# Moving the weight-only half of a Hyena mixer into an earlier feed-forward stage

## The reference, cut to what matters

```
h = _rms_norm(x, norm_mlp_pre[l])                       # first block, end of layer l (l = 0, 1)
u = square(relu(h @ w_up[l]))                           # 256 x 4096
x = x + _rms_norm(u @ w_down[l], norm_mlp_post[l])

feats, t = hyena_position_features(seq)                 # 256 x 33: constants
hdn = sin(freq * (feats @ w1 + b1)); hdn = sin(freq * (hdn @ w2 + b2)); hdn = sin(freq * (hdn @ w3 + b3))
h = (hdn @ w_out) * exp(-t * abs(deltas))               # 256 x 4096: 2 orders x (fwd, bwd) x 1024 channels
fwd, bwd = h[:, :, 0], h[:, :, 1]
circ = concatenate([fwd, zeros, flip(bwd[1:])])         # 512 lags
filt = circ / (sum(abs(circ)) + RMS_EPS)

proj = x @ w_in; x1, x2, v = dwconv_centred(xv); gate    # Hyena mixer
z = x1 * (fft_long_conv(v, filt[:, 0]) + skip[0] * v)    # product of spectra, length 512
y = x2 * (fft_long_conv(z, filt[:, 1]) + skip[1] * z)
return y * silu(gate)
```

## Time and profile before

| | us |
|---|---|
| median of the runs | 1590.55 |
| the profiled execution's own time | 1594.65 |
| its span, first to last instruction | 1593.3 |
| TensorE busy | 1495.4 (94%) |
| VectorE busy | 1060.4 (67%) |
| ScalarE busy | 777.4 (49%) |

### The profile page before, as it was taken

How to read it: one execution, slowest core, us unless ns; L and a number is a source line. 1 busy time by engine, 2 the same in 40 slices (tenths; PEclk the granted TensorE clock), 3 DMA queues, 4 the chain that set the end, 5 groups by cost and what they waited for, 6 DMA issues and landing times.

```text
span 1593.3 us, 27504 instructions
## 1 busy us (share of the span) xinstructions
PE 1495.4 (94%) x11820; PEld 1319.0 (83%) x11820; DVE 1060.4 (67%) x1830; ACT 777.4 (49%) x1318; POOL 51.7 (3%) x58
## 2 busy tenths in 40 slices
PE   7999999999999998989999999897789999999998
PEld 7888898899989998988999898886678878885566
DVE  5576666655564776656555586757467668977877
ACT  4656444544454565445445566343242436746435
POOL 0001011000000010110000000000000000000000
PEclk9999999999999999989999999998779799999999
DMA  8554344565546543434655564200000266432143
GB/s 274 182 179 137 106 133 146 181 221 197 185 159 190 187 141 115 133 121 150 205 186 195 175 217 129 86 26 1 1 2 3 108 213 190 144 107 66 53 127 131
DMA packets 151190, 219.13 MB, mean 138 GB/s; under 512 B 6228, under 2 KB 110684, under 8 KB 150428
## 3 DMA queue, kind: packets, MB, share of 16 engines
q1 hardware_dynamic: 151068, 217.37, 42.0%
HBM read 216.29 MB, written 1.06 MB: 136 GB/s over the span
## 4 chain that ended last, share of the span: by engine, by line
PE 72%; DVE 16%; ACT 8%; DMA 2%; issue 1%; SPq 0%; DVEq 0%; ACTq 0%
PE bank L396 18%; PE bank L398 18%; PE bank L397 18%; DVE weights_low L372 4%; PE bank L3684 2%; ACT weights_high L359 2%; PE bank L2200 1%; PE bank L2158 1%; PE bank L898 1%; PE bank L2095 1%; PE bank L3694 1%; DMA place<-w_in_dram 1%; PE bank L3705 1%; DVE place L1240 1%; PE bank L2402 1%
## 5 line engine op out<-in xcount | busy, mean ns | idle before, releaser
L372 DVE TENSOR_TENSOR weights_low<-place,weights_high 128x1024 fp32r<-128x1024 f32 (+2 forms) x387 | 449.3, 1205 | 165.7 <-ACT weights_high L359 165.1
L359 ACT ACTIVATE weights_high<-place 128x1024 fp32r<-128x1024 f32 (+2 forms) x387 | 378.7, 1032 | 124.3 <-DMA place<-w_down_dram 40.7
L396 PE MATMUL bank<-hT_high,weights_high 128*128 128x256 f32 x1152 | 327.2, 284 | 3.2 <-DVE hT_low L493 2.1
L397 PE MATMUL bank<-hT_low,weights_high 128*128 128x256 f32 x1152 | 321.2, 279 | 0.0
L398 PE MATMUL bank<-hT_high,weights_low 128*128 128x256 f32 x1152 | 321.0, 279 | 0.0
L396 PEld LDWEIGHTS bank<-hT_high,weights_high 128*128 128x128 f32 x1152 | 218.9, 190 | 7.1 <-DVE hT_low L493 2.9
L397 PEld LDWEIGHTS bank<-hT_low,weights_high 128*128 128x128 f32 x1152 | 218.6, 190 | 0.6
L398 PEld LDWEIGHTS bank<-hT_high,weights_low 128*128 128x128 f32 x1152 | 218.4, 190 | 0.0
L398 PE MATMUL bank<-weights_high,branchT_low 128*128 128x512 f32 x256 | 100.8, 394 | 0.0
L397 PE MATMUL bank<-weights_low,branchT_high 128*128 128x512 f32 x256 | 100.4, 392 | 0.0
L396 PE MATMUL bank<-weights_high,branchT_high 128*128 128x512 f32 x256 | 99.6, 389 | 0.3
(11 more groups left out here) (441 smaller groups left out, 3157.1 us busy)
## 6 DMA issues: line engine op xcount, KB each, us to landing
place<-w_in_dram SPq DMA_DIRECT2D x48, 1024.0 KB, 5.3
place<-w_up_dram SPq DMA_DIRECT2D x32, 1024.0 KB, 5.3
place<-w_down_dram SPq DMA_DIRECT2D x32, 1024.0 KB, 4.9
place<-even_w_in_dram SPq DMA_DIRECT2D x17, 1024.0 KB, 5.2
place<-w_out_dram SPq DMA_DIRECT2D x16, 1024.0 KB, 5.0
place<-odd_w_in_dram SPq DMA_DIRECT2D x16, 1024.0 KB, 5.7
place<-w_branch_dram SPq DMA_DIRECT2D x12, 1024.0 KB, 5.0
place<-ple_gate_dram SPq DMA_DIRECT2D x8, 1024.0 KB, 5.7
```

The costliest lines, as they stand in the source:

```text
L359: nc.scalar.activation(high[:, lo:hi], self.raw[p % SLOTS][:, lo:hi], ACT.Copy).then_inc(*A("high", p, j))
L372: nc.vector.tensor_tensor(low[:, lo:hi], self.raw[p % SLOTS][:, lo:hi], high[:, lo:hi].bitcast(FP32), ALU.subtract).then_inc(*V())
L396: nc.tensor.matmul(out, left[0], right[0], start=first, stop=False)
L397: nc.tensor.matmul(out, left[0], right[1], start=False, stop=False)
```

## The change

The small network, the filters, their sums and norms and their spectra are computed in the first block's last feed-forward stage. After each of its 32 pieces (step m) each engine runs `filters_tensor`, `filters_vector` or `filters_scalar` with that m: passes of the network at m = 0 to 2, then four units (order n, channel half hf) that start at steps 4, 10, 16 and 22 and take ten steps each. They use banks 6 and 7, and SBUF that is free after attention. Each unit's spectra (five tiles of 512) are stored to DRAM and loaded back in the Hyena stage, just into the place where they were computed before. The inverse sums stay in SBUF.

The spectra are now taken of folded lags: lag j and lag 256 - j share a row (the tables `feats` and `minus_t` are permuted, and VectorE forms sums and differences), so that a tile takes one matmul over 128 rows, not two. Lag 0 and lag 128 need a row of their own: the first goes with row 0, the other comes in as a matmul of one row by 512 for tiles 0 and 4. A unit so has seven spectrum matmuls, where it had ten.

In the Hyena stage these functions go, the signal's spectra get places of their own, and the blanks and `hold` go. The first signals are computed inside the loop over pieces (n = 8 and 10), the first product right behind the last convolution. `tables_odd` shrinks from 2,691 to 1,152 columns; the filter tables (899 columns) are loaded in the feed-forward stage.

```diff
@@ mlp_tensor (the same lines stand in mlp_vector and mlp_scalar)
             k.pair(("up", l, i, j), ("up", l, i, j), f.hT, k.turned("normed", "mlp", l), bank=4 + j)
+            if l + 1 == DEPTH:
+                filters_tensor(k, f.filters, 4 * i + j)
...
             T.same("down_done", l, i, j)
+            if l + 1 == DEPTH:
+                filters_tensor(k, f.filters, 4 * i + 2 + j)
@@
+UNIT_AT = [4 + 6 * u for u in range(len(HY_UNITS))]
+def filters_sync(k, h, l):
...
+    filter_load(k, h, 0)
+    for m in range(4 * TURNS):
+        k.load_up_to_piece(k.piece["up", l, 0, 0] + m)
+        if m + 1 in UNIT_AT[1:]:
+            filter_load(k, h, UNIT_AT.index(m + 1))
+        if m - 14 in UNIT_AT:
+            spectra_store(k, h, *HY_UNITS[UNIT_AT.index(m - 14)])
+    k.load_beyond(("down", l, TURNS - 1, 1))
+    spectra_store(k, h, *HY_UNITS[-1])
+def filter_load(k, h, u):
...
+        SP.wait_ge(("filter", *before, 1, TT - 1), ("filter_decay", *before, 1, TT - 1))
+def spectra_store(k, h, n, hf):
+    SP.wait_ge(("free", "spectrum", n, hf, SPECTRUM[-1]))
...
+def filters_tensor(k, h, m):
+    if m < 3:
+        hidden_tensor(k, h, m)
+    for u, (n, hf) in enumerate(HY_UNITS):
+        at = m - UNIT_AT[u]
+        if at in (0, 1):
+            filter_tensor(k, h, n, hf, at)
+        elif at == 4:
+            sums_tensor(k, h, n, hf)
+            spectrum_tensor(k, h, n, hf, 3)
+        elif at == 5:
+            skips_tensor(k, h, n, hf)
+            spectrum_tensor(k, h, n, hf, 2)
+        elif at == 8:
+            spectrum_tensor(k, h, n, hf, 1)
+            spectrum_tensor(k, h, n, hf, 0)
+        elif at == 9:
+            spectrum_tensor(k, h, n, hf, 4)
+def spectrum_tensor(k, h, n, hf, tile):
...
+    ins = nc.tensor.matmul(b, split(k.table("dft_filter"), 5, P)[:, tile, :], h.E[:, tile % 4, :], start=True, stop=whole)
+    if not whole:
+        ins = nc.tensor.matmul(b, k.table("ones")[0:1, :], h.E[0:1, 1, :], start=False, stop=True)
+def filters_vector(k, h, m):   # network at m < 3; at 0, 1 filter; 3 magnitudes and fold; 4 sums; 5 skip row
...
+def filters_scalar(k, h, m):
+    if m < 3:
+        k.sine_scalar(("hid", m), h.hid, h.sine[0:HY_F, 2, :])
+    # at -1, 0 exponentials; 2 magnitudes; 4, 5, 8, 9 the copies of spectra from PSUM
...
@@ even_sync
-    SP.wait_ge(("layer_done", DEPTH - 1))
+    SP.wait_ge(("layer_done", DEPTH - 1), ("spectra_stored", *HY_UNITS[-1]))
@@ odd_sync
+    for (n, hf), piece in zip(HY_UNITS, ((0, 1), (0, 3), (1, 1), (1, 3))):
+        k.load_up_to(("hy", *piece))
+        SP.wait_ge(("spectra_stored", n, hf))
+        nc.sync.dma_start(o.H[n][:, hf].rearrange("p a b -> p (a b)"), dram["spectra"][n, hf]
+                          ).then_inc(*k.spectra_loaded[n, hf]("spectra_loaded", n, hf))
@@ odd_tensor
+        if n in (7, 9):
+            norm_tensor(k, o, 0, n // 2 - 3)
+        if n in (8, 10):
+            signal_tensor(k, o, 0, n // 2 - 4)
...
     inverse_tensor(k, o, 0, 0)
+    norm_tensor(k, o, 1, 0)
     k.token_major(("silu", "hy", 1), k.halves_of(("silu", "hy", 1)), o.hT, WB, h_ready)
     inverse_tensor(k, o, 0, 1)
+    norm_tensor(k, o, 1, 1)
     signal_tensor(k, o, 1, 0)
     signal_tensor(k, o, 1, 1)
     inverse_tensor(k, o, 1, 0)
@@ odd_vector
+        if n in (8, 10):
+            weigh_by_norm_vector(k, o, 0, n // 2 - 4)
+        if n in (6, 8):
+            fold_vector(k, o, 0, n // 2 - 3)
+        if n == 11:
+            product_vector(k, o, 0, 0)
     k.low_of_next()
     product_vector(k, o, 0, 1)
+    k.low_of_next()
     gate_tokens_vector(k, o, 0, 0)
+    weigh_and_gate_vector(k, o, 0)
     gate_tokens_vector(k, o, 0, 1)
     weigh_and_gate_vector(k, o, 1)
     product_vector(k, o, 1, 0)
@@ product_vector (the scratch place is now shared by both halves)
-    V.wait_ge(("signal", n, hf, 3))
+    V.wait_ge(("signal", n, 1, 3))
```

More of the change, by code:

```diff
@@ L51 @@
 HY_ORDER, HY_SHORT, HY_EMB, HY_F = 2, 3, 33, 64
+HY_UNITS = [(n, hf) for n in range(HY_ORDER) for hf in range(2)]
 HY_XV = 3 * D
@@ L139, in offsets @@
         at = start
+        if which == "filters":
+            at += sum(a.shape[1] for a in sets["even"].values())
         for name, a in tables.items():
@@ new lines, in hidden_tensor, with filter_tensor @@
+def hidden_tensor(k, h, j):
+    nc, T, n = k.nc, k.T, (HY_EMB, HY_F, HY_F)[j]
+    b = k.claim("hid", j, bank=6)
+    T.wait_ge(("filters_loaded",), *([("sine", "hid", j - 1)] if j else []))
+    nc.tensor.matmul(b[0:HY_F, 0:S], h.w123[0:n, j, :], h.hid if j else k.table("feats")[0:n, :], start=True, stop=True
+                     ).then_inc(*T("hid", j))
+def filter_tensor(k, h, n, hf, f):
+    nc, T = k.nc, k.T
+    for t in range(TT):
+        b = k.claim("filter", n, hf, f, t, bank=6 + t)
+        T.wait_ge(("filter_loaded", n, hf), ("sine", "hid", 2))
+        nc.tensor.matmul(b, h.hid[:, t * P:(t + 1) * P], h.w[0:HY_F, f, :], start=True, stop=True).then_inc(*T("filter", n, hf, f, t))
@@ new lines, in sums_tensor, with skips_tensor @@
+def sums_tensor(k, h, n, hf):
+    nc, T = k.nc, k.T
+    b = k.claim("sums", n, hf, bank=6)
+    T.wait_ge(("mag_summed", n, hf))
+    for j in range(4):
+        ins = nc.tensor.matmul(b[:, j:j + 1], h.mag[:, 0, 0, j * P:(j + 1) * P], k.table("ones")[:, 0:1], start=True, stop=True)
+    ins.then_inc(*T("sums", n, hf))
+def skips_tensor(k, h, n, hf):
+    nc, T = k.nc, k.T
+    b = k.claim("skips", n, hf, bank=6)
+    T.wait_ge(("over_filter_sums", n, hf))
+    for j in range(4):
+        ins = nc.tensor.matmul(b[0:1, j * P:(j + 1) * P], h.skips[:, n, 4 * hf + j:4 * hf + j + 1], k.table("ident"), start=True, stop=True)
+    ins.then_inc(*T("skips", n, hf))
@@ new lines, in sums_vector @@
+def sums_vector(k, h, n, hf):
+    nc, V = k.nc, k.V
+    of = slice(4 * hf, 4 * hf + 4)
+    sums, skips = h.sums[:, n, of], h.skips[:, n, of]
+    V.wait_ge(("sums", n, hf))
+    nc.vector.tensor_scalar(sums, k.bank("sums", n, hf)[:, 0:4], EPS_RMS, None, ALU.add).then_inc(*V("free", "sums", n, hf))
+    V.wait_ge(V)
+    nc.vector.tensor_tensor(skips, sums, h.skip[:, n, of], ALU.mult).then_inc(*V())
+    V.wait_ge(V)
+    nc.vector.reciprocal(sums, sums).then_inc(*V("over_filter_sums", n, hf))
@@ new lines, in mag_scalar, with spectrum_scalar @@
+def mag_scalar(k, h, n, hf):
+    nc, A = k.nc, k.A
+    if (n, hf) != HY_UNITS[0]:
+        before = HY_UNITS[HY_UNITS.index((n, hf)) - 1]
+        A.wait_ge(("sums", *before), ("passed_by", *before))
+    A.wait_ge(("filter_made", n, hf, 1))
+    nc.scalar.activation(h.first, h.ft[0:1, 0, 0, :], ACT.Copy).then_inc(*A("first_kept", n, hf))
+    nc.scalar.activation(h.mag, h.ft, ACT.Abs).then_inc(*A("mag", n, hf))
+def spectrum_scalar(k, h, n, hf, tile):
+    nc, A = k.nc, k.A
+    if tile == SPECTRUM[0] and (n, hf) != HY_UNITS[0]:
+        A.wait_ge(("spectra_stored", *HY_UNITS[HY_UNITS.index((n, hf)) - 1]))
+    A.wait_ge(("spectrum", n, hf, tile))
+    nc.scalar.activation(h.H[:, tile, :], k.bank("spectrum", n, hf, tile), ACT.Copy).then_inc(*A("free", "spectrum", n, hf, tile))
@@ L3511, in odd_pieces @@
         k.by_rows(("silu", "hy", hf), w_in, HY_XV + hf * WB)
-    k.blank()
-    k.blank()
     close_pieces(k, 1)
-    for half in range(2):
-        k.hold(("ple_w", 1, half), ("gated", HY_ORDER - 1, 1, TT - 1))
 def odd_sync(k, o):
```

439 lines of the change are left out of this document (184 added, 255 removed).

## The result

The changed kernel is slower by some 1.7%: the ratio is 1.0171 with an interval of 1.0133 to 1.0208. One of its four runs, 5385.96 us, was disturbed and is left out; the others took 1615.1, 1621.37 and 1626.18, against a median of 1592.47 for four runs of the kernel before (three of them gave the 1590.55 above). The profiled execution took 1626.18 with a span of 1624.6, so it stands 31.3 above the span of before. I forecast 1606 with a range to 1616: the sign was right, the size was not.

The account below looks back on a forecast made before the run. TensorE was taken to end last in both the feed-forward and Hyena stages. Terms 48.4 - 1.7 + 3.7 + 6.6 + 3.1 - 49.5 + 5.6 - 1.1 = +15.1 us gave 1606 on the median, range 1583 to 1616.

Parts of the forecast that it names:

- Added matmuls, 48.4: Feed-forward stage: filters, sums, skips, network and spectra lengthen full TensorE by 48.4 us.
- the choice to charge a one-row matmul like any other: Feed-forward stage: eight new one-row, 512-wide spectrum matmuls cost 0.86 us each, as height saves nothing.
- a second step that failed: Feed-forward stage: added matmuls charged at their row times, with no term for breaks between weight pieces.
- The step that failed: Feed-forward stage, SP's queue: unit weight loads and spectra stores ahead of weight pieces cost nothing.
- third rival: Feed-forward stage stalls on stores ahead of weight pieces or ScalarE's wait for a spectrum copy: +9 us, 1615; chance 0.12.
- Network waits, 3.7: Feed-forward stage: TensorE waits 0.5 and 3.3 us for the small network's successive passes, 3.7 in the sum.
- Layer's end, 6.6 and 3.1 of half clock: End of feed-forward stage: closing norm 6.6 us later behind last spectrum, copy and table load; idle TensorE's half clock loses 3.1.
- E + 9.5: End of feed-forward stage: closing norm done 9.5 us after the last down product ends, against E + 2.9 before.
- Hyena, -49.5 + 5.6: Hyena stage: output projection starts 49.5 us sooner without the moved work; half clock in the tail costs 5.6.
- the close, -1.1: Close of the even block: smaller odd tables shorten ScalarE's 3.57 us wait for a gate piece by 1.1.
- VectorE decides in the tail: Hyena tail after the last pair: VectorE sets the pace; TensorE idles from T + 41.3 to 45.2, then 2.0 and 2.6.

Follow-up runs that it names:

- the probe: Kernel before, with unused matmuls behind every second weight piece of the feed-forward stage: a break cost 0.3 to 0.4 us at some places, none at others.
- end_early: Changed kernel with the last unit's last three spectra one step earlier, none behind the last down product: ratio 1.0135.
- stays_apart_tail: Last unit's spectra in Hyena, earlier stores, spaced network passes; against that, last three spectra grouped and output projection's first cut earlier: feed-forward stage 3.7 us slower.

## Why the prediction was wrong in size

- **Added matmuls, 48.4.** Their own starts add up to 47.9 over the stage (per unit: filters 3.82, sums 0.81, skips 0.95, spectra 5.97; network 1.7). Right, and the choice to charge a one-row matmul like any other was right: it took 1.05. What I left out is the breaks, which I put at nothing without a reason, and that is a second step that failed: the pieces behind them are together 8.6 longer. The rows were of blocks that stand together; here they stand in 26 places between pieces. That is 0.3 a place, within what the probe shows for a break (0 to 0.4); a probe of each kind of place was not made, so this part is argued from the size.
- **The step that failed: "Both waits are over about when the piece ahead of them could be issued, so they cost nothing".** I looked at what waits on SP, and not at who waits for SP's store: ScalarE's first copy of the next unit. 6.3 us of TensorE's waits and 3.5 of half clock behind two of them, 9.8. Two edits that take away the wait alone, a second place or an earlier store, gave 10.4 each, near that sum. My third rival had this mechanism ("a store ahead of a weight piece ... or ScalarE waiting for a spectrum copy with a cut behind it", three at 1.5 and three loads, +9) and 0.12. That its 9 comes near the measured 9.8 is luck: the three unit loads cost TensorE nothing, and three waits of 2.1 with the half clock make up the sum. What ScalarE waited for was a store that had not landed, with the cut behind it; no wait of TensorE there goes back to a late weight piece.
- **Network waits, 3.7.** 2.7 (0.2 and 2.5), with 1.2 of half clock behind.
- **Layer's end, 6.6 and 3.1 of half clock.** 7.0 and about none: the clock did fall there, but over the turns, which wait for ScalarE and VectorE anyway; the first column pieces took 118 ns a matmul, as before. The path was right: both tiles' norms in a row behind the last copy, laid out as E + 9.5 and measured as E + 10.1. It was only in the expectation of end_early that I took the copy alone for the cause.
- **Hyena, -49.5 + 5.6, and the close, -1.1.** -44.6 from first pair to end; the close took 36.0 from its first ple piece to Hyena, 37.3 before. Right, and for the reason given: VectorE decides in the tail (its longest wait 4.2, forecast 3.9), and the clock fell to a mean of 0.85 there. The even block as a whole was 0.7 longer all the same, within its scatter.

Sum of the stage: 54.5 for matmuls and breaks (45.9 without the last spectrum, 8.6), 3.9 network, 9.8 store, 7.0 end, -0.4 at its entry: 74.8 of the measured 74.9. With the failed step's 9.8 the forecast would have been 1616, with 54.5 for 46.7 as well 1624, and with the end's 2.7 too many taken off 1621; the middle one of the three runs took 1621.37.

## What to carry to other kernels

A transfer that leaves a buffer has two waits: the one ahead of it, and the one of whoever fills the buffer next; follow both, and on the second ask what else stands in that engine's queue. Moving work out of a stage gives back only what the next engine allows, and into a full stage it costs its full price and, at most places where it is put, a break (0.3 us here); leave the part for which the old stage has idle time. Where work is added at the end of a stage, look for what had been done early there, as the first tile's norm.

## What the runs showed that I had not expected

- The granted clock is not fixed by the pattern alone. Behind the same three waits of about 2 us it was 0.84, 1.00 and 0.84 over the 11 us that follow in the changed kernel, and 1.00 all three times in the kernel with the last spectra two steps earlier (waits of 1.88, 2.14, 2.12). In these runs half clock behind such a wait is a chance of 1.7 us a time, not a term.
- It can fall with TensorE busy throughout: in the probe, over four one-row matmuls (first row) and the up pieces behind them (windows; clock behind GpSimd's count).

```profile
846.00:851.00 5.00, 5.00 (x11) 1.75 (x10) 2.36 (x2) 1.85 (x2) 0.00 (x0) 0.80 0.56 210
851.00:858.00 7.00, 7.00 (x43) 7.00 (x44) 0.00 (x0) 0.00 (x0) 0.00 (x0) 0.66 0.00 0
```

In stays_apart_tail, where a unit's last spectra (three matmuls of 128 rows, two of one) stand in one group, it fell behind one of the three groups (0.76 over the 7.2 us from 894.2, with TensorE busy throughout and in the 5.2 us before) and stayed at 1.00 behind the other two.

- A matmul of one row, 512 wide in plain fp32, took 1.05 us where one of 128 rows took 0.88.
- The table load at the layer's end took 1.28 us and the next operation started 0.01 behind it (989.83, 991.12). The Trainium skill, "ScalarE: Activation LUTs", What ACT_TABLE_LOAD costs, adds a drain of 1.38 to each switch; no run here shows it, so the estimate by the page would have been that much too late.
